# Expert layer of a hybrid encoder step: gate/up products with the weights stationary, downs and one-hot products by pair

## The chip, the core and the metric

One Trainium2 chip, one of its NeuronCores; everything runs in one launch. The metric is the time of the core in microseconds (us), smaller is better.

## The reference

One layer: adaLN, an input projection, an RWKV-7 branch and a gated linear attention branch, a merge, and then a hierarchical mixture of 32 experts on 544 rows (512 prompt, 32 sample) of 1024 numbers, all float32. The change concerns the experts only. Every row chooses two of the 32 experts:

```python
for e in range(N_EXPERTS):
    hid = jax.nn.silu(ht @ e_gate[e]) * (ht @ e_up[e])        # (T, 512)
    out = out + combine[:, e:e + 1] * (hid @ e_down[e])       # (T, 1024)
x = x + gt2 * out                                             # then the final RMS norm
```

The gate and up matrices of an expert are 1024x512, the down matrix 512x1024: 2 MB (a "unit") each, 96 units in all.

## The kernel before, in words

The stages before the experts (input projection, both branches, merge, `w_out`, router) are not touched, but for the layout of a few small tiles. The router ranks the rows of each expert and gives each a slot. A **round** does 64 slots (`BLK`) of every expert; with the inputs of the reference one round is enough. Experts go in 16 **pairs** (`NP`). For a pair, GpSimd gathers 128 rows from DRAM into `x_blk` (`gather`, L2124), 64 for each expert. Then, on TensorE (the loop is `a_round` of the tensor block, from L2754):

- `rows_turned` (products on L2672): eight 128x128 transposes; VectorE copies them to `x_t` (`rows_copied`, L3058), 8 blocks of [128 of the model dimension, 128 slots], in two buffers.
- `gate_up(e)` (L2711): the stationary operand is `x_t[:, k]` of the expert's 64 slots (128x64), the moving operand is 512 columns of gate or up weights. Gate goes to PSUM partitions 0 to 63, up to 64 to 127, 16 products in pairs of column halves. VectorE copies the result to `gu` (`gate_up_copied`, L3065).
- `hidden_turned(e)` (L2724): four 128x128 transposes of `gu`, so that the hidden dimension lies on the partitions; ScalarE makes the silu (L2485), VectorE multiplies by up (`hidden`, L3070) into `hid`.
- `down(e)` (L2736): stationary `hid[:, f]` (128x64), moving 512 columns of down weights, 8 products; the two halves of the 1024 outputs go to the two halves of the partitions. VectorE multiplies by the row's weight times `gt2` (`coef`, `down_scaled`, L3084), ScalarE rounds that to fp32r (L2491) and VectorE makes the rest (L3087).
- `rows_added(pair, j)` (L2689): for each of five row tiles, one-hot matrices (64 slots x 128 rows, made by `one_hots` on VectorE) times the two fp32r parts for both experts of the pair, 8 products; VectorE adds the result to `x2` (`rows_summed`, L3111). They are spread over the k loop of the next pair's odd `gate_up` (`PRODUCTS_AT`).
- The last pair has its own end: `last_down` (L2750), `last_added` (L3117), norm (`normed`, L3126, squares on ScalarE) and the stores (L2236).

The order on TensorE is written out by hand: `gate_up(e + 1)`, then `down(e)`, then `hidden_turned(e + 1)`. The units stream through eight buffers; SyncE's queue issues the load of unit n (L2025) once unit n - 8 has been used (`gu_mm`, `dn_mm`), and TensorE waits for `wg_in`, `wd_in`. A float32 product is carried out as two MATMUL instructions, each behind a LDWEIGHTS of its own; a product of fp32r operands is one of each.

Of the kernel before, what the change touches and what calls it, by code (L numbers as in the profile page):

```python
# [13 lines left out]
P = 128  # L14
# [25 lines left out]
def build(nc, I, O):  # L40
    ctx = ExitStack()
    with ctx:
# [1804 lines left out]
        tmp = Region(LOWER + 4 * D + 256, LOWER + MID - 4 * D)  # L1847
# [7 lines left out]
        ROW_WORDS = 2 * 5 * P + 4 * 512  # L1855
# [51 lines left out]
        E_LAST = NE - 2  # L1907
# [19 lines left out]
        gt2_h = Region(base + D).take(2, 512)  # L1927
# [13 lines left out]
        slot_w = route.take(2, NE)  # L1941
# [18 lines left out]
        tgt = small.take(NE)  # L1960
# [17 lines left out]
        act_g = low.take(4, BLK)  # L1978
        hid = low.take(4, BLK)
        gu = [Region(pos_oh_at + 512 * s).take(512) for s in range(2)]  # L1980
        after_units = Region(LOW_UNIT + 8 * D, rhs_at)
        moe_r = Region(LOWER, LOWER + ROW_WORDS)
        oh_t = moe_r.take(2, 5, P)
        y_parts = [[moe_r.take(512) for _ in range(2)] for _ in range(2)]
        after_r = Region(LOWER + ROW_WORDS, ARENA - 24 * D)
        x_t = [after_r.take(KD, 2 * BLK) for _ in range(2)]
        code_rows = [after_r.take(5, P), after_units.take(5, P)]
        y_full = after_units.take(512)
        consts_over = Region(summing_at, summing_at + 1200)
        coef = [consts_over.take(512) for _ in range(2)]  # L1990

        def y_of(e):

            return x_blk[:, 512 * (e % 2):512 * (e % 2) + 512] if e >= E_LAST else y_full

# [3 lines left out]
        STREAM = [("gate", 0), ("up", 0)]  # L1999
        for e in range(NE):  # L2000
            STREAM += [("gate", e + 1), ("up", e + 1)] * (e + 1 < NE) + [("down", e)]
# [14 lines left out]
        wg_in = [sem(f"wg_in{s}") for s in range(3)]  # L2016
        wd_in = [sem(f"wd_in{s}") for s in range(3)]
# [4 lines left out]
        def load_unit(sp, n):  # L2022
            kind, e = STREAM[n]
            source, landed = {"gate": (egate, wg_in), "up": (eup, wg_in), "down": (edown, wd_in)}[kind]
            sp.dma_start(weights_of(kind, e), source[e]).then_inc(landed[e % 3], 16)  # L2025
# [93 lines left out]
        def weights_kept(v, r, table):  # L2119
            v.wait_ge(slot_w_mm, r + 1)  # L2120
            nc.vector.tensor_copy(slot_w.rearrange("p a e -> p (a e)"), table[:, 0:2 * NE]).then_inc(slot_w_done, 1)
# [9 lines left out]
        gu_out = sem("gu_out")  # L2131
        gu_tr = sem("gu_tr")
# [11 lines left out]
        oh_done = sem("oh_done")  # L2144
        yh_done = sem("yh_done")
        yrest_done = sem("yrest_done")
        moe_mm = sem("moe_mm")
# [9 lines left out]
        DN_USES = [len(range(s, NE, 3)) for s in range(3)]  # L2157
        ADDS = 5 * (NP - 1)
        GU_USES = [len(range(s, NE, 3)) for s in range(3)]
# [14 lines left out]
        with nc.Block() as block:  # L2174
            @block.sync
            def _(sp):
# [24 lines left out]
                for s in range(2):  # L2201
                    for b in range(2):
                        sp.dma_start(gt2_h[BLK * b:BLK * b + BLK, s, :],
                                     mod_dram[s, 5 * D + 512 * b:5 * D + 512 * b + 512].partition_broadcast(BLK)
                                     ).then_inc(last_rows_in, 16)
# [8 lines left out]
                def a_round(r):  # L2214
                    if not first(r):
                        sp.wait_ge(dn_mm, r * NE)
                        sp.sem_inc(held, 1)
                        sp.wait_ge(y_final, r * 80)
                        sp.sem_inc(held, 1)
                        for n in range(8):  # L2220
                            load_unit(sp, n)
                    for n in range(8, len(STREAM)):
                        kind, e = STREAM[n - 8]
                        sp.wait_ge(dn_mm if kind == "down" else gu_mm, r * NE + (e + 1))
                        if n == len(STREAM) - 1:
                            sp.wait_ge(dn_mm, r * NE + (NE - 3))
                        load_unit(sp, n)
                    sp.wait_ge(gu_mm, r * NE + (NE - 1))
                    sp.sem_inc(held, 1)
                    sp.wait_ge(dn_mm, r * NE + (NE - 2))  # L2230
# [13 lines left out]
            def _(pool):  # L2244
# [46 lines left out]
                for b in range(2):  # L2291
                    half = slice(BLK * b, BLK * b + BLK)
                    i = iota_i[half, 0:NE].bitcast(I32)
                    step(pool.iota(i, pattern=[[int(CODE), NE]], base=int(CODE), channel_multiplier=1))
                    step(pool.tensor_copy(tgt[half], i))
# [14 lines left out]
                def a_round(r):  # L2310
                    if not first(r):
                        pool.wait_ge(idx_done, r * 2 + 2)
                        pool.wait_ge(x_tr9, r * NE)
                        pool.wait_ge(last_mm, r * 5)
# [7 lines left out]
            def _(act):  # L2322
# [138 lines left out]
                for k in range(2):  # L2461
                    nc.scalar.activation(code_rows[k][:, 0:4, :].rearrange("p i t -> p (i t)"), bank(6 + k), ACT.Copy
                                         ).then_inc(code_out, 1)
                for k in range(2):
                    nc.scalar.activation(code_rows[k][:, 4, :], bank(4)[:, k * P:(k + 1) * P], ACT.Copy
                                         ).then_inc(code_out, 1)

                def coef_of_prompt(r, e):
                    s = e % 2
                    if e >= 2:  # L2470
                        act.wait_ge(y_done, r * NE + (e - 1))
                    else:
                        act.wait_ge(slot_w_done, r + 1)
                    if e == 0 and first(r):
                        act.wait_ge(last_rows_in, 64)
                    nc.scalar.activation(coef[s], gt2_h[:, 0, :], ACT.Copy, scale=slot_w[:, 0, e:e + 1]
                                         ).then_inc(coef_half, 1)

                def a_round(r):
                    for e in range(2):  # L2480
                        coef_of_prompt(r, e)
                    for e in range(NE):
                        s = e % 2
                        act.wait_ge(gu_tr, r * NE + (e + 1))
                        nc.scalar.activation(act_g, psum[2][:, 0, :].rearrange("p (f t) -> p f t", f=4)[:, :, 0:BLK],  # L2485
                                             ACT.Silu).then_inc(silu_done, 1)
                        if 1 <= e < NE - 1:
                            coef_of_prompt(r, e + 1)
                        if e < E_LAST:
                            act.wait_ge(y_done, r * NE + (e + 1))  # L2490
                            nc.scalar.activation(y_parts[s][0], y_full, ACT.Copy).then_inc(yh_done, 1)  # L2491
# [12 lines left out]
            def _(pe):  # L2504
# [153 lines left out]
                for k in range(2):  # L2658
                    for i in range(5):
                        row = bank(6 + k)[:, i * P:(i + 1) * P] if i < 4 else bank(4)[:, k * P:(k + 1) * P]  # L2660
                        m = mm(row, code[:, k, i:i + 1].broadcast_to([P, P]), ident, start=True, stop=True)
                m.then_inc(code_mm, 1)

                def rows_turned(r, p):
                    pe.wait_ge(x_in9, r * (NP * 16) + 16 * p + 16)
                    for h in range(2):
                        if p:
                            pe.wait_ge(x_t9, r * NE + (2 * p + h - 1))
                        elif not first(r):
                            pe.wait_ge(x_t9, r * NE)  # L2670
                        for k in range(4):
                            m = nc.tensor.transpose(psum[h][:, 0, k * P:(k + 1) * P],  # L2672
# [3 lines left out]
                PRODUCTS_AT = [1, 3, 5, 7]  # L2676

                def rows_added(r, pair, j):
                    n = 5 * pair + j
                    if j == 0:  # L2680
                        pe.wait_ge(yrest_done, r * E_LAST + (2 * pair + 2))
                        pe.wait_ge(oh_done, r * NE + (2 * pair + 2))
                    if n:
                        pe.wait_ge(moe_added, r * ADDS + n)
                    for h in range(2):
                        for part in range(2):
                            for b in range(2):
# [6 lines left out]
                def gate_up(r, e):  # L2694
                    s = e % 2
                    pair = e // 2 - 1 if s and e >= 3 else None
                    if e == NE - 1:
                        for j in range(5):
                            rows_added(r, pair, j)
                    pe.wait_ge(x_t9, r * NE + (e - s + 2))  # L2700
                    pe.wait_ge(wg_in[e % 3], r * (32 * GU_USES[e % 3]) + 32 * (e // 3) + 32)
                    if e >= 2:
                        pe.wait_ge(gu_out, r * NE + (e - 1))
                    elif not first(r):
                        pe.wait_ge(x3_done, r * 5)
# [489 lines left out]
```

## Time and profile before

| | us |
|---|---|
| median of 3 runs | 1511.84 (1511.11 to 1514.94) |
| the profiled execution, its own time | 1509.26 |
| its span in the profile | 1507.5 |
| issue of the first unit, start of the first gate/up product in that span | 961.7, 993.2 |
| mean granted TensorE clock | 0.975 |
| busy: TensorE matmul / VectorE / ScalarE | 1400.7 / 722.2 / 473.9 |

A granted clock of 1 is 2.4 GHz, 0.5 is 1.2 GHz. The expert stage is the stretch from 991 us to the end; a pair takes 30.67 us there.

### The profile page before, as it was taken

The numbers are of one execution on the slowest core, as the hardware profiler recorded it, in microseconds if no ns is written. First come the engines' busy times: TensorE is split into PE (matmuls) and PEld (weight loads), VectorE is DVE, ScalarE is ACT, GpSimd is POOL, SyncE is SP. The second block draws the span as 40 slices with busy tenths as digits, with TensorE's granted clock in tenths as the row PEclk, the third lists the DMA queues.
The fourth block names the chain that finished last, engine by engine and source line by source line (L and its number), as shares of the span: only waits on it lengthen the run. The fifth ranks groups of instructions, "written<-read, shape, count | busy, mean of one in ns | idle before, by whom it ended". The sixth has DMA issues, their size and how long they took to land. (4 is left out here: it accounts for less than half of the span.)

```text
span 1507.5 us, 31643 instructions
## 1 busy us (share of the span) xinstructions
PE 1400.7 (93%) x14017; PEld 1015.6 (67%) x14017; DVE 722.2 (48%) x1184; ACT 473.9 (31%) x764; POOL 167.2 (11%) x200
## 2 busy tenths in 40 slices
PE   5899999999999998888879999799999999999986
PEld 1778999999998987777779998653333333333332
DVE  3322134652235456556555666624555554554545
ACT  2333345554554543333335442110100110011002
POOL 2000000010112124324201101000000000000000
PEclk9999999999999998999999999789999999999988
DMA  8656422234432210000422461499999999999951
GB/s 313 195 187 222 139 72 71 83 110 130 124 90 60 68 44 11 4 5 4 135 56 74 163 213 63 198 407 426 427 426 427 425 427 426 427 426 425 426 232 61
DMA packets 124510, 310.01 MB, mean 206 GB/s; under 512 B 12407, under 2 KB 97617, under 8 KB 109010
## 3 DMA queue, kind: packets, MB, share of 16 engines
q1 hardware_dynamic: 113680, 285.07, 49.8%
q10 hardware_dynamic: 7522, 15.57, 2.9%
q0 software_dynamic: 3168, 7.30, 1.3%
q8 instruction: 113, 1.85, 0.5%
q14 instruction: 27, 0.22, 0.0%
HBM read 299.06 MB, written 12.79 MB: 207 GB/s over the span
## 5 line engine op out<-in xcount | busy, mean ns | idle before, releaser
L838 PE MATMUL bank<-upper2end 128*128 128x272 f32 x3168 | 419.2, 291 | 5.4 <-DVE upper2end L1079 5.4
L838 PEld LDWEIGHTS bank<-upper2end 128*128 128x128 f32 x3168 | 403.4, 189 | 27.5 <-issue 26.2
L1056 DVE TENSOR_TENSOR upper2end<-upper,upper2end 128x1024 fp32r<-128x1024 f32 x66 | 81.7, 1238 | 286.3 <-ACT upper2end L604 286.2
L2711 PE MATMUL bank<-upper7b 128*64 128x512 f32 x784 | 208.0, 603 | 1.0 <-DVE upper7b L3058 1.0
L2491 ACT ACTIVATE upper_r7b<-lower 128x512 fp32r<-128x512 f32 x30 | 18.9, 629 | 407.4 <-DVE lower L3084 407.4
L3111 DVE TENSOR_TENSOR lower<-lower,bank 128x1024 f32<-128x1024 f32 (+1 forms) x75 | 91.4, 1218 | 97.2 <-PE bank L2689 97.2
L2711 PEld LDWEIGHTS bank<-upper7b 128*64 128x64 f32 x784 | 57.7, 137 | 96.9 <-issue 93.0
L2689 PEld LDWEIGHTS bank<-upper_r7b 64*128 64x128 f32 x600 | 52.5, 191 | 86.5 <-DVE lower L3111 58.6
L2689 PE MATMUL bank<-upper_r7b 64*128 64x512 f32 x600 | 93.2, 430 | 18.0 <-DVE lower L3111 9.6
L2543 PE MATMUL bank<-upper_r 128*128 128x272 f32 x768 | 103.0, 294 | 3.2 <-DVE upper_r L2958 3.2
L2543 PEld LDWEIGHTS bank<-upper_r 128*128 128x128 f32 x768 | 99.4, 191 | 5.9 <-DVE upper_r L2790 3.6
L2736 PE MATMUL bank<-upper7b,lower 128*64 128x512 f32 x368 | 83.5, 595 | 0.0
L2711 PE MATMUL bank<-lower,upper7b 128*64 128x512 f32 x240 | 81.4, 602 | 0.0
L604 ACT ACTIVATE upper2end<-upper 128x1024 fp32r<-128x1024 f32 x66 | 69.6, 1054 | 11.0 <-ACT upper L633 6.5
L2124 POOL DMA_INDIRECT lower<-expert_in,lower x16 | 16.0, 1001 | 427.0 <-PE bank L2672 385.1
L3084 DVE TENSOR_TENSOR lower<-bank,lower 128x512 f32<-128x512 f32 x32 | 22.1, 692 | 79.3 <-PE bank L2736 79.3
L2736 PEld LDWEIGHTS bank<-upper7b,lower 128*64 128x64 f32 x368 | 25.4, 137 | 47.1 <-issue 45.7
L2575 PE MATMUL bank<-upper_r 128*128 128x512 f32 x192 | 48.0, 407 | 0.0
L3065 DVE COPY lower<-bank 128x512 f32<-128x512 f32 x32 | 22.0, 688 | 49.6 <-PE bank L2711 49.6
L1442 ACT ACTIVATE upper<-bank 128x512 f32<-128x512 f32 x36 | 21.5, 597 | 74.2 <-DVE upper L1518 74.1
L789 PE MATMUL bank<-lower 128*32 128x512 f32 x184 | 29.3, 703 | 15.7 <-DMA lower<-in_w_ada 15.7
L2575 PEld LDWEIGHTS bank<-upper_r 128*128 128x128 f32 x192 | 36.7, 194 | 9.3 <-issue 1.1
(412 smaller groups left out, 1904.0 us busy)
## 6 DMA issues: line engine op xcount, KB each, us to landing
upper7b<-in_expert_w_gate SPq DMA_DIRECT2D x25, 2048.0 KB, 20.3
upper7b<-in_expert_w_up SPq DMA_DIRECT2D x24, 2048.0 KB, 21.9
upper7b<-in_expert_w_down SPq DMA_DIRECT2D x23, 2048.0 KB, 17.0
upper<-in_w_in SPq DMA_DIRECT2D x66, 512.0 KB, 3.9
lower<-in_w_ada SPq DMA_DIRECT2D x23, 1024.0 KB, 5.0
lower<-in_expert_w_down SPq DMA_DIRECT2D x9, 2048.0 KB, 16.3
lower<-in_expert_w_up SPq DMA_DIRECT2D x8, 2048.0 KB, 23.3
lower<-in_expert_w_gate SPq DMA_DIRECT2D x7, 2048.0 KB, 20.8
```

The costliest lines, as they stand in the source:

```text
L604: nc.scalar.activation(w_high[u % 2], w_slot[u % 2], ACT.Copy).then_inc(w_high_done, 1)
L789: m = mm(acc[32 * b:32 * b + 32, :], c_t[:, k, :], w[:, b * 512:(b + 1) * 512], start=k == 0, stop=k == KD - 1)
L838: m = mm(psum[s][:, c, 0:HALF], w_part[s][:, k, :], h_part[:, k, c * HALF:(c + 1) * HALF], start=k == 0 and w_part is w_high and h_part is ...
L1056: ve.tensor_tensor(w_rest[u % 2], w_slot[u % 2], w_high[u % 2].bitcast(F32), ALU.subtract).then_inc(w_split, 1)
L2543: m = mm(psum[s][:, c, 0:HALF], w[s][:, k, :], cols(y[b][:, k], c), start=k == 0 and w is wb_high and y is y_high, stop=k == KD - 1 and w ...
L2575: m = mm(psum[OUT_BANKS[i]][:, b, :], m_part[:, k, t], w[:, b * 512:(b + 1) * 512], start=k == 0 and m_part is m_high and w is not wo_rest[k],
L2689: m = nc.tensor.matmul(psum[3][:, b, :], oh_t[half, h, AT[j], :], y_parts[h][part][half, :], start=h + part == 0, stop=h + part == 2)
L2711: m = nc.tensor.matmul(psum[s][64 * b:64 * b + 64, 1, :], x_t[(e // 2) % 2][:, k, s * BLK:(s + 1) * BLK], w[:, k, :], start=k == 0, stop=k ...
L2736: m = nc.tensor.matmul(psum[2][64 * b:64 * b + 64, 1, :], hid[:, f, :], w[:, f, b * 512:(b + 1) * 512], start=f == 0, stop=f == 3)
L3065: ve.tensor_copy(gu[s], psum[s][:, 1, :]).then_inc(gu_out, 1)
L3084: ve.tensor_tensor(y_of(e), psum[2][:, 1, :], coef[s], ALU.mult).then_inc(y_done, 1)
L3111: ve.tensor_tensor(x2[0:n, j, :], x2[0:n, j, :], psum[3][0:n].rearrange("t b c -> t (b c)"), ALU.add).then_inc(moe_added, 1)
```

## The change

Gate and up weights become the stationary operand (128x128 blocks, their columns taken with a step of four words), the 64 slots of `x_t` the moving one. The products then come out with the hidden dimension on the partitions: `gu`, its copy and `hidden_turned` go; silu reads PSUM, `hidden` multiplies with PSUM. A `gate_up` is 64 products with 64 moving columns in place of 16 with 512.

```diff
-                    gate_and_up = weights_of("gate", e), weights_of("up", e)
-                    for k in range(KD):
-                        if pair is not None and e < NE - 1 and k in PRODUCTS_AT:
-                            rows_added(r, pair, PRODUCTS_AT.index(k))
-                        for b, w in enumerate(gate_and_up):
-                            m = nc.tensor.matmul(psum[s][64 * b:64 * b + 64, 1, :],
-                                                 x_t[(e // 2) % 2][:, k, s * BLK:(s + 1) * BLK], w[:, k, :],
-                                                 start=k == 0, stop=k == KD - 1)
+                    for n, kind in enumerate(("gate", "up")):
+                        pe.wait_ge(*landed(r, kind, e))
+                        w = weights_of(kind, e).rearrange("p k (n q) -> p k q n", q=4)
+                        for q in range(4):
+                            at = 4 * BLK * n + BLK * q
+                            for k in range(KD):
+                                m = nc.tensor.matmul(bank(2 + s)[:, at:at + BLK], w[:, k, q, :],
+                                                     x_t[:, k, s * BLK:(s + 1) * BLK], start=k == 0, stop=k == KD - 1)
+                            if q == 3:
+                                m.then_inc(gu_mm, 1)
+                            if e >= 2 and 8 * s + 4 * n + q in PRODUCTS_AT:
+                                rows_added(r, e // 2 - 1, PRODUCTS_AT.index(8 * s + 4 * n + q))
```

The two downs of a pair are done together, expert 0 on partitions 0 to 63 and expert 1 on 64 to 127, both halves of the outputs in one two-bank tile; scaling, rounding and the rest are then done once per pair on 128x1024. The one-hot matrix holds 128 slots, and a tile needs 4 products in place of 8:

```diff
+                    for f in range(4):
+                        for b in range(2):
+                            for s in range(2):
+                                m = nc.tensor.matmul(psum[2][64 * s:64 * s + 64, b, :], hid[s][:, f, :],
+                                                     w[s][:, f, b * 512:(b + 1) * 512], start=f == 0, stop=f == 3)
...
-                    for h in range(2):
-                        for part in range(2):
-                            for b in range(2):
-                                half = slice(BLK * b, BLK * b + BLK)
-                                m = nc.tensor.matmul(psum[3][:, b, :], oh_t[half, h, AT[j], :],
-                                                     y_parts[h][part][half, :], start=h + part == 0,
-                                                     stop=h + part == 2)
+                    for part in range(2):
+                        for b in range(2):
+                            m = nc.tensor.matmul(psum[3][:, b, :], oh_t[:, j * P:(j + 1) * P],
+                                                 y_parts[part][:, b * 512:(b + 1) * 512], start=part == 0,
+                                                 stop=part == 1)
```

The order on TensorE, the order of the units and the pair's end become:

```diff
+                    for p in range(NP):
+                        gate_up(r, 2 * p)
+                        gate_up(r, 2 * p + 1)
+                        if p < P_LAST:
+                            rows_turned(r, p + 1)
+                        down(r, p)
+                    for j in range(5):
+                        last_rows_added(r, j)
...
+        for e in range(0, NE, 2):
+            STREAM += [("gate", e), ("up", e), ("gate", e + 1), ("up", e + 1), ("down", e), ("down", e + 1)]
...
+                PRODUCTS_AT = [4, 6, 8, 10, 12]
```

Beside that `x_t` has one buffer, each of the eight unit buffers a semaphore of its own, a gate unit is released as soon as the gate products are done, `gt2` is broadcast to 128 partitions (two loads of 512 KB for four of 128 KB), and the last pair goes the way of the others: rounded and rest parts made by halves (`last_scaled`, `last_rounded`), then four fp32r products for each tile (`last_rows_added`) in place of `last_down`'s float32 ones.

## Rows read from the trace of the kernel before

**Rows 1.** The page: what the DMA engines moved, GB/s in 40 equal slices of the span.
```profile
GB/s 313 195 187 222 139 72 71 83 110 130 124 90 60 68 44 11 4 5 4 135 56 74 163 213 63 198 407 426 427 426 427 425 427 426 427 426 425 426 232 61
```

**Rows 2.** Busy time by stretch, core 0: one pair of the expert stage.
```profile
core 0: us, PE busy (x) PEld busy (x) DVE busy (x) ACT busy (x) POOL busy (x), PEclk, DMA share, GB/s
...
1100.80:1131.47 30.67, 29.87 (x154) 11.74 (x152) 15.85 (x21) 3.02 (x6) 0.99 (x1) 1.00 1.01 427
```

**Rows 3.** Waits of SyncE's queue, 1020 to 1440 us: us in total, times, longest.
```profile
SPq L2025 <- PE bank L2711: 285.3, 28, 13.0
```

**Rows 4.** Issue to landing of the units (L2025): 1000 to 1200, then 1300 to 1456 us.
```profile
DMA to landing us min/median/max: 15.2/20.9/26.3
...
DMA to landing us min/median/max: 13.0/18.5/24.0
```

**Rows 5.** Timeline of PE (start, us, what, xcount): first gate/up, transposes, down, hidden transposes.
```profile
993.21 7.09 PE L2711 MATMUL bank<-upper7b 128*64 128x512 f32 x32 [1.01 <-DVE upper7b L3058]
...
1100.80 1.16 PE L2672 MATMUL bank<-lower 128*128 128x128 f32 x8
1101.89 3.65 PE L2736 MATMUL bank<-lower 128*64 128x512 f32 x16
1105.47 0.75 PE L2724 MATMUL bank<-lower 128*128 128x128 f32 x4
```

**Rows 6.** Groups of PE and VectorE in the pair of Rows 2: one-hot products and their adds.
```profile
line engine op names shapes xcount | busy us, mean ns | idle before us <-releasers
...
L2689 PE MATMUL bank<-upper_r7b 64*128 64x512 f32 x42 | 6.4, 415 | 0.8 <-DVE upper_r7b L3087 0.5 <-DVE lower L3111 0.3
L3111 DVE TENSOR_TENSOR lower<-lower,bank 128x1024 f32<-128x1024 f32 x4 | 4.9, 1220 | 5.6 <-PE bank L2689 5.6
```

**Rows 7.** Router burst, 36 columns moving: its loads in the timeline, then by line (min/median/max ns).
```profile
938.92 1.64 PEld L2604 LDWEIGHTS bank<-lower 128*128 128x128 f32 x14
...
L2604 PEld LDWEIGHTS bank<-lower x15: 192/192/193, 938.8 to 940.4; 128*128 128x128 f32 x15
```

**Rows 8.** Timeline of a burst of float32 loads whose products move 128 columns.
```profile
386.76 0.98 PEld L950 LDWEIGHTS bank<-lower,upper 128*128 128x128 f32 x8
```

**Rows 9.** Groups by line and shape: fp32r products of 272 columns.
```profile
L838 PE MATMUL bank<-upper2end 128*128 128x272 f32 x3168 | 419.2, 291 | 5.4 <-DVE upper2end L1079 5.4
```

**Rows 10.** Timeline of PE: fp32r products of 512 columns, weights 128x128.
```profile
940.52 8.60 PE L2575 MATMUL bank<-upper_r 128*128 128x512 f32 x36
```

**Rows 11.** Timeline of the last hidden tile: silu on ScalarE, product on VectorE.
```profile
1482.99 0.38 ACT L2485 ACTIVATE lower<-bank 128x256 f32<-128x256 f32 x1 [26.55 <-PE bank L2724]
...
1483.41 0.42 DVE L3070 TENSOR_TENSOR lower<-lower,bank 128x256 f32<-128x256 f32 x1 [0.39 <-ACT lower L2485]
```

**Rows 12.** Timeline after a down: scaling on VectorE, rounding on ScalarE.
```profile
1443.07 0.69 DVE L3084 TENSOR_TENSOR lower<-bank,lower 128x512 f32<-128x512 f32 x1 [2.27 <-PE bank L2736]
1443.79 0.63 ACT L2491 ACTIVATE upper_r7b<-lower 128x512 fp32r<-128x512 f32 x1 [18.05 <-DVE lower L3084]
```

**Rows 13.** Timeline of VectorE at the end: last down scaled, first tile added.
```profile
1487.92 0.69 DVE L3084 TENSOR_TENSOR lower<-bank,lower 128x512 f32<-128x512 f32 x1 [3.43 <-PE bank L2736]
1489.93 1.22 DVE L3117 TENSOR_TENSOR lower<-lower,bank 128x1024 f32<-128x1024 f32 x1 [1.31 <-PE bank L2750]
```

**Rows 14.** Busy time by stretch (columns of Rows 2): router, end, and RWKV recurrence.
```profile
967.00:991.00 24.00, 20.57 (x98) 19.94 (x96) 7.47 (x43) 2.76 (x5) 1.76 (x2) 0.51 1.01 423
...
1459.00:1472.00 13.00, 9.04 (x36) 4.84 (x38) 4.58 (x4) 0.00 (x0) 0.00 (x0) 0.50 0.00 0
...
586.00:731.00 145.00, 122.77 (x4714) 110.37 (x4712) 87.21 (x180) 54.03 (x103) 54.60 (x42) 1.00 0.04 12
```

**Rows 15.** Timeline of PE at the end of the router, at the lower clock.
```profile
980.17 4.48 PE L2092 MATMUL bank<-lower 128*128 128x32 f32 x20 [2.12 <-DVE lower L3047]
...
986.59 4.61 PE L2661 MATMUL bank<-lower 128*128 128x128 f32 x20
```

More of the change, by code:

```diff
@@ L1940, in build @@
         code = route.take(2, 5)
[L1941 removed]
+        slot_w = route.take(2, NP)
         oh_both = route.take(2, 5, NE)
@@ L1977, in build @@
         low = Region(base + 4 * D, LOW_UNIT)
-        act_g = low.take(4, BLK)
-        hid = low.take(4, BLK)
-        gu = [Region(pos_oh_at + 512 * s).take(512) for s in range(2)]
+        hid = [low.take(4, BLK) for _ in range(2)]
         after_units = Region(LOW_UNIT + 8 * D, rhs_at)
+        act_g = after_units.take(4 * BLK)
+        coef = Region(base + D).take(D)
+        y_full = Region(pos_oh_at).take(D)
         moe_r = Region(LOWER, LOWER + ROW_WORDS)
[L1983 to L1988, printed above, removed]
+        oh_t = moe_r.take(5 * P)
+        y_parts = [moe_r.take(D) for _ in range(2)]
+        x_t = Region(LOWER + ROW_WORDS + 2 * D, ARENA - 24 * D).take(KD, 2 * BLK)
         consts_over = Region(summing_at, summing_at + 1200)
-        coef = [consts_over.take(512) for _ in range(2)]
-        def y_of(e):
-            return x_blk[:, 512 * (e % 2):512 * (e % 2) + 512] if e >= E_LAST else y_full
+        code_rows = [consts_over.take(T) for _ in range(2)]
         UNIT = 4 * D
@@ L1998, in build @@
         UNIT_AT = [experts_at + n * UNIT for n in range(1, 7)] + [LOW_UNIT + UNIT, LOW_UNIT]
-        STREAM = [("gate", 0), ("up", 0)]
-        for e in range(NE):
-            STREAM += [("gate", e + 1), ("up", e + 1)] * (e + 1 < NE) + [("down", e)]
+        STREAM = []
+        for e in range(0, NE, 2):
+            STREAM += [("gate", e), ("up", e), ("gate", e + 1), ("up", e + 1), ("down", e), ("down", e + 1)]
         unit_no = {kind_e: n for n, kind_e in enumerate(STREAM)}
@@ L2156, in build @@
         ROUNDS_MAX = (T + BLK - 1) // BLK
-        DN_USES = [len(range(s, NE, 3)) for s in range(3)]
         ADDS = 5 * (NP - 1)
-        GU_USES = [len(range(s, NE, 3)) for s in range(3)]
+        P_LAST = NP - 1
+        LAST_BANKS = (3, 0, 1, 2, 3)
         NORM_AT = {j: (2 * j + 1, 2 * j + 2) for j in range(5)}
@@ L2479, in a_round, with coef_of_prompt @@
-                def a_round(r):
[L2480 to L2491, printed above, removed]
+                def coef_of_prompt(r, p):
+                    if p:
+                        act.wait_ge(y_done, r * P_LAST + p)
+                    else:
+                        act.wait_ge(slot_w_done, r * 2 + 2)
+                        if first(r):
+                            act.wait_ge(last_rows_in, 32)
+                        else:
+                            act.wait_ge(y_last, r * 2)
+                    nc.scalar.activation(coef, gt2_b[:, 0, :], ACT.Copy, scale=slot_w[:, 0, p:p + 1]
+                                         ).then_inc(coef_half, 1)
@@ L2658, in _ @@
                 for k in range(2):
-                    for i in range(5):
-                        row = bank(6 + k)[:, i * P:(i + 1) * P] if i < 4 else bank(4)[:, k * P:(k + 1) * P]
-                        m = mm(row, code[:, k, i:i + 1].broadcast_to([P, P]), ident, start=True, stop=True)
+                    for j, n in TILES:
+                        row = bank(6 + k)[:, j * P:(j + 1) * P] if j < 4 else bank(4)[:, k * DEC:(k + 1) * DEC]
+                        m = mm(row, code[:, k, AT[j]:AT[j] + 1].broadcast_to([P, P]), ident[:, 0:n], start=True,
+                               stop=True)
                 m.then_inc(code_mm, 1)
@@ L2718, in hidden_turned @@
-                def hidden_turned(r, e):
-                    s = e % 2
-                    pe.wait_ge(gu_out, r * NE + (e + 1))
-                    if e == 0 and first(r):
-                        pe.wait_ge(code_out, 4)
-                    for f in range(4):
-                        m = nc.tensor.transpose(psum[2][:, 0, f * P:(f + 1) * P],
-                                                gu[s].rearrange("t (p k) -> t k p", p=P)[:, f, :], ident)
-                    m.then_inc(gu_tr, 1)
-                def down(r, e):
-                    pe.wait_ge(hid_done, r * NE + (e + 1))
-                    pe.wait_ge(wd_in[e % 3], r * (16 * DN_USES[e % 3]) + 16 * (e // 3) + 16)
-                    if e >= 1:
-                        pe.wait_ge(y_done, r * NE + e)
-                    w = weights_of("down", e)
-                    for f in range(4):
-                        for b in range(2):
-                            m = nc.tensor.matmul(psum[2][64 * b:64 * b + 64, 1, :], hid[:, f, :],
-                                                 w[:, f, b * 512:(b + 1) * 512], start=f == 0, stop=f == 3)
-                    m.then_inc(dn_mm, 1)
@@ L2747, in last_down @@
                     pe.sem_inc(held, 1)
-                    for b in range(2):
-                        half = slice(BLK * b, BLK * b + BLK)
-                        m = nc.tensor.matmul(psum[j % 4][0:n, b, :], oh_t[half, i, AT[j], 0:n].bitcast(F32),
-                                             y_of(E_LAST + i)[half, :], start=i == 0, stop=stop)
-                    return m
+                    for part, ready in enumerate((yh_last, yrest_last)):
+                        for b in range(2):
+                            if j == 0:
+                                pe.wait_ge(ready, r * 2 + (b + 1))
+                            m = nc.tensor.matmul(psum[LAST_BANKS[j]][:, b, :], oh_t[:, j * P:(j + 1) * P],
+                                                 y_parts[part][:, b * 512:(b + 1) * 512], start=part == 0,
+                                                 stop=part == 1)
+                    m.then_inc(last_mm, 1)
                 def a_round(r):
```

276 lines of the change are left out of this document (131 added, 145 removed).

## The prediction, as put on record before the changed kernel was run

> **What bounds the kernel now.** I looked first for the stage that the change touches. From 991 us on the experts run, a third of the span, and there the page shows the DMA engines flat at 425 to 427 GB/s [rows 1], which looks like a bound by weight traffic. The busy times by stretch show more: one pair takes 30.67 us, the pairs before and after it take the same, TensorE is busy 29.87 us of it and its clock is whole [rows 2]. So TensorE, too, is full. The waits tell which of the two leads: the queue that issues the units waits for the gate/up products, 285.3 us in 420 [rows 3], while no wait of TensorE for a load is listed. The landings say the same: a unit lands 20.9 us after its issue early in the stage and 18.5 us late in it [rows 4]; the loads gain on TensorE a little. TensorE sets the pair at 30.67 us, and DMA is just behind: 26.3 us against 24.0 us at most over some ten pairs [rows 4] puts it some 0.2 to 0.3 us a pair lower, about 30.4. That is the floor: whatever TensorE saves in a pair, hardly more than 0.3 us of it can show, and whatever it gains in work shows in full.
>
> **The pair before, on TensorE.** A gate/up is 32 instructions in 7.09 us to the end of the last, some 6.9 us to the next instruction; two of them run side by side in the two column halves, so a pair of instructions takes 0.43 us [rows 5]. Transposes 1.09, a down 3.58 from start to start, hidden transposes 0.75 or 0.7 to the next start [rows 5]. Twice 6.9, 3.5 and 0.7, and 1.1, make 23.3 us; the remaining 7.4 are the five one-hot groups (6.4 busy [rows 6]) and the switches around them.
>
> **Gate/up after: the term that decides.** Per expert 64 products of 64 moving columns, each float32 and so two instructions: 128 loads of 128x128 weights and 128 matmuls, 256 of each per pair. Before it was 64 instructions per pair, two at a time. The arithmetic is the same, but the array was filled from the long side; now the load has the 128 columns and the matmul only 64. What such a load costs is in the router: there float32 weights of 128x128 meet only 36 moving columns. 14 loads take 1.64 us, the last one 0.192, so they follow at (1.64 - 0.19) / 13 = 0.111 us at the full clock [rows 7]. With 128 columns moving the pace is (0.98 - 0.19) / 7 = 0.113 [rows 8]. From 36 to 128 columns nothing changes: the load is the bound, and the matmul hides under it. 64 lies between, so I take 0.112: 256 x 0.112 = 28.7 us per pair, against 13.8 before. Bounds: the least that rows 7 leave is 0.107 (27.4 us); above, the fp32r products pace at 419.2 / 3168 = 0.132 with 272 columns [rows 9], of which I allow 0.125 (32.0 us), because the new loads step over four words and no row with many such loads shows their price when nothing longer hides it.
>
> At one place a page speaks differently. The Trainium skill, "TensorE: Matmul & The Clock Gate", section "Back-to-back issue gap", has a stream of load and matmul pairs at about 81 ns with 128 moving columns; the trace has 0.113 us for the same columns in float32 [rows 8], and the measurement decides. By the page's figure gate/up would be an estimated 20.7 us per pair.
>
> **The other parts, per pair.**
> - Hidden transposes (8 instructions, 1.4 us) and two copies of `gu` go. VectorE's work falls, but it was busy only 15.85 of 30.67 us [rows 2]: worth nothing by itself.
> - One-hot products: 20 instructions of 512 columns in place of 40 that ran in pairs. Full-height fp32r products pace at (8.60 - 0.40) / 35 = 0.234 [rows 10]: 4 are 0.94, with the switch 0.98, five 4.9 us. They wait for the adds (1.22 us [rows 6]), but two blocks of eight products, 3.6 us, lie between two groups: hidden. The first comes after five blocks, 9 us; scaling, rounding and rest of 128x1024 take about twice 0.69, 0.63 and 0.69 [rows 12], 4 us: hidden.
> - Transposes of the next inputs, 1.1 us, unchanged. `x_t` has one buffer now; its copies (1.3 us) run under the down of 7 us.
> - Down: 16 products, 32 instructions, again two at a time: twice the 16 of [rows 5], 6.95 us. Before it, `hid` of the second expert must be there: silu 0.38, product 0.42 [rows 11], with drain and hops 1.25 us after the last gate/up product, of which the transposes cover 1.1: 0.2 us.
> - Loads: six units per pair in 41.8 us are 300 GB/s, below what ran before; they land early. The wider `gt2` rows put 0.5 MB ahead of two units (1.2 us), and those are needed 30 us later: nothing. `coef` on ScalarE stands before the first silu, but both are due only 14 us into the stage.
>
> Sum: 28.7 + 4.9 + 1.1 + 0.2 + 6.95 = 41.85 us a pair, 11.2 more than 30.67. The first pair has no one-hot products: 36.9.
>
> **The ends.** The stage starts as before, at 993.2 [rows 5]; router and code products keep their loads. The last down ends at 993.2 + 36.9 + 15 x 41.85 = 1657.9. Before, the first add came 2.0 us after it [rows 13]; now two scalings, a rounding, two rests by halves and two more products stand in the chain: 0.69 + 0.69 + 0.04 + 0.69 + 0.69 [rows 12] and some 0.6, 3.4 us. From the first add to the end is 1507.5 - 1489.9 = 17.6 us [rows 13], led by adds and norms that don't change. The old kernel's bare one-hot groups at the lower clock before its last gate/up (1459 to 1472 [rows 14]) go, which the count of pairs contains. Span 1657.9 + 3.4 + 17.6 = 1678.9. The profiled execution took 1509.26 for a span of 1507.5: 1680.7; the median lies 2.6 higher: **1683 us**.
>
> **Rivals.**
> - *The loads hide, DMA is the floor (faster).* If the 64-column matmul set the pace (0.43 us is four times 128 columns, so 64 take about 0.055) or one load served both instructions, gate/up would be some 14 us, TensorE's pair 27 to 28 us, under the 30.4 of DMA. It decides from 0.068 us per instruction down. Then 96 units and the gathers, 209 MB at 427 GB/s, run from the first issue at 962 to 1453; a down, the new chain and the end (28 us) give a span of 1481, 1486 us in all. Against it: each of the matmuls in rows 7 and 8 has its own load, at 0.111. Chance 0.05.
> - *A pace between, about 0.08.* Gate/up 20.7, pair 33.8, by the same sum 1558 us. The page's 81 ns above is this case, worked out here from the pair of rows; rows 7 speak against it. Chance 0.05.
> - *The clock falls.* Before the experts TensorE worked without a stop on loads with 32 columns moving, 967 to 991 us, at a granted clock of 0.51 [rows 14]: 20 such instructions took 4.48 us, 0.22 each [rows 15]. The clock was whole again only after 20 products of 128 columns [rows 15]. The new gate/up is between: as many cycles of load as two of matmul. If the clock stays at 1.2 GHz, gate/up is 256 x 0.215 = 55 us, with products and downs partly at half speed a pair is some 74: about 2195 us. Against it: in the RWKV recurrence thousands of short products, down to 32 columns, with matmuls busy 123 of 145 us, kept 1.00 [rows 14]; and each pair ends in 7 us of dense downs. Chance 0.10, of a mild form (some pairs) within it.
>
> **How the numbers follow.** The forecast has 0.80. Its range: 0.107 takes 16 x 256 x 0.005 = 20 us off, smaller waits 8 more; 0.125 adds 53 and waits 8: 1655 to 1745. The rivals lie outside and hold the 0.20 left. A measurement of this kernel can tell about 0.3% (4.5 us) from no change. Slower: 0.80 + 0.05 + 0.10, less a little; faster: 0.05; a pace that lands on no change: 0.01.
>
> **What would show it.** Right: the pair is 41 to 43 us; gate/up matmuls start every 0.112 us, and weight loads are busy nearly all of gate/up where they were 11.7 of 30.7; the GB/s fall from 427 to about 310; the queue waits for TensorE still more; granted clock 1.00. Wrong: a pace of 0.055 with GB/s at 427 (first rival), 0.08 (second), PEclk 0.5 in gate/up (third). If the pace is 0.112 and the pair still over 43, a wait that I put at nothing is there: before a down for `hid`, or before a one-hot group for `yrest_done`. A pace far above 0.125 at a full clock would mean that the four-word step of the weights costs.

## The result, and the profile after

The changed kernel takes 2265.25 us (median of 4 runs, 2263.54 to 2266.86) against 1511.97: the ratio is 1.498, 95% interval 1.495 to 1.500. The profiled execution took 2266.47 us for a span of 2264.7. The forecast was 1683, in a range of 1655 to 1745; the direction was right, and the size was wrong by 582 us.

The page of the changed kernel: span, busy time, clock and DMA in 40 slices, and the costliest groups (line engine op out<-in, shapes, xcount | busy us, mean ns | idle before).

```profile
span 2264.7 us, 36761 instructions
PE 2170.1 (96%) x16641; PEld 1948.5 (86%) x16641; DVE 681.0 (30%) x1078; ACT 472.5 (21%) x735; POOL 180.5 (8%) x200
...
PEclk9999999999999899955555555555555555555556
...
L2703 PEld LDWEIGHTS bank<-upper7b 128*128 128x128 f32 x3072 | 728.7, 329 | 20.7 <-issue 8.9
L2703 PE MATMUL bank<-upper7b 128*128 128x64 f32 x3072 | 723.8, 435 | 1.0 <-DVE upper7b L3044 1.0
```

The weight loads, busy two thirds of the span before, are busy 86% of a longer one, and the mean clock in the expert stage is 0.56 (1500 to 2000 us). At first sight this is the forecast's third rival (the clock falls, 2195 us). From the first input transposes of one pair to those of the next is a pair, and the starts of the groups between give its parts:

```profile
1446.41 1.92 PE L2686 MATMUL bank<-lower 128*128 128x128 f32 x8
...
1524.89 1.91 PE L2686 MATMUL bank<-lower 128*128 128x128 f32 x8
```

```profile
1502.86 2.05 PE L2733 MATMUL bank<-upper_r7b 128*128 128x512 f32 x4
1504.71 7.52 PE L2703 MATMUL bank<-upper7b,lower 128*128 128x64 f32 x32
...
1526.73 8.60 PE L2720 MATMUL bank<-upper7b,lower 128*64 128x512 f32 x32
1535.26 18.93 PE L2703 MATMUL bank<-upper7b 128*128 128x64 f32 x80
```

A pair is 78.5 us, where it was 30.67 [rows 2] and 41.85 was forecast. From start to start a one-hot group is 1.85 us (forecast 0.98), the down 8.5 (6.95), the transposes 1.8 (1.1). Taking these off, 78.5 - 9.25 - 8.5 - 1.8 = 58.9 us are left for gate/up, forecast 28.7. So 30 of the 36.6 us that the pair is over its forecast are gate/up.

The row that decides what slowed it stands right behind a down, where the clock had just been raised. Busy times by stretch (core 0: us, PE, PEld, DVE, ACT, POOL busy, clock, DMA share, GB/s), and the timeline of the loads in the first of the two:

```profile
1536.00:1539.80 3.80, 3.80 (x18) 3.80 (x18) 1.83 (x2) 2.10 (x2) 0.00 (x0) 1.00 0.94 310
1541.00:1603.00 62.00, 62.00 (x252) 60.07 (x251) 6.51 (x6) 0.38 (x1) 0.00 (x0) 0.50 0.37 142
```

```profile
1535.94 4.06 PEld L2703 LDWEIGHTS bank<-upper7b 128*128 128x128 f32 x17
```

At a granted clock of 1.00 the loads follow at (4.06 - 0.33) / 16 = 0.233 us, not 0.112. At 0.50 they take the same: 32 instructions in 7.52 us, (7.52 - 0.44) / 31 = 0.228. (The two figures differ by how the runs are cut; over 80 instructions that begin in the first stretch it is (18.93 - 0.44) / 79 = 0.234.) A load whose time doesn't change with the clock isn't slow because of the clock. What sets these loads apart from those of [rows 7] and [rows 8] is their step of four words. That the step makes them slow is theory S below; theory C, its rival, is that the fallen clock does.

### The profile page after: what moved, and what is told of

Its sections match the earlier page's. It is cut to its first block, busy times and chain, and to the rows that moved or that the text cites. A ratio compares the mean times of both kernels' runs of the same rounds, so it can differ in the third digit from the quotient of the medians.

```text
span 2264.7 us, 36761 instructions
## 1 busy us (share of the span) xinstructions
PE 2170.1 (96%) x16641; PEld 1948.5 (86%) x16641; DVE 681.0 (30%) x1078; ACT 472.5 (21%) x735; POOL 180.5 (8%) x200
## 4 chain that ended last, share of the span: by engine, by line
PE 64%; DVE 1%; ACT 0%; issue 0%; ACTq 0%; DVEq 0%
PE bank L2703 42%; PE bank L2733 6%; PE bank L2720 6%; PE bank L2556 4%; PE bank L2588 2%; PE bank L2686 1%; PE bank L2540 1%; PE bank L2617 0%; DVE upper7b L3112 0%; DVE lower L3103 0%; PE bank L2082 0%; PE bank L2090 0%; PE bank L2537 0%; PE bank L2674 0%; PE bank L2603 0%
## 5 line engine op out<-in xcount | busy, mean ns | idle before, releaser
L2703 PEld LDWEIGHTS bank<-upper7b 128*128 128x128 f32 x3072 | 728.7, 329 | 20.7 <-issue 8.9
L2703 PE MATMUL bank<-upper7b 128*128 128x64 f32 x3072 | 723.8, 435 | 1.0 <-DVE upper7b L3044 1.0
L2703 PEld LDWEIGHTS bank<-upper7b,lower 128*128 128x128 f32 x1024 | 243.5, 329 | 7.1 <-issue 3.2
L2703 PE MATMUL bank<-upper7b,lower 128*128 128x64 f32 x1024 | 241.9, 435 | 0.0
L2733 PE MATMUL bank<-upper_r7b 128*128 128x512 f32 x300 | 154.1, 665 | 0.0
L2125 POOL DMA_INDIRECT lower<-expert_in,lower x16 | 29.0, 1810 | 1079.7 <-PE bank L2686 991.0
L2720 PE MATMUL bank<-upper7b,lower 128*64 128x512 f32 x384 | 101.6, 689 | 0.0
L2733 PEld LDWEIGHTS bank<-upper_r7b 128*128 128x128 f32 x300 | 88.7, 326 | 14.5
L3050 DVE TENSOR_TENSOR lower<-lower,bank 128x256 f32<-128x256 f32 x32 | 13.5, 421 | 255.7 <-ACT lower L2484 255.7
L2488 ACT ACTIVATE upper_r7b<-lower 128x1024 fp32r<-128x1024 f32 x15 | 15.9, 1057 | 165.2 <-DVE lower L3078 165.2
L2588 PEld LDWEIGHTS bank<-upper_r 128*128 128x128 f32 x192 | 36.6, 194 | 9.2 <-issue 1.1
```

Source lines behind the costliest of these rows:

```text
L2125: pool.indirect_dma_start(x_blk, None, h2_dram, bass.IndirectOffsetOnAxis(ap=as_u32(x_idx[:, p:p + 1]), axis=0), bounds_check=T - 1, oob_i ...
L2588: m = mm(psum[OUT_BANKS[i]][:, b, :], m_part[:, k, t], w[:, b * 512:(b + 1) * 512], start=k == 0 and m_part is m_high and w is not wo_rest[k],
L2703: m = nc.tensor.matmul(bank(2 + s)[:, at:at + BLK], w[:, k, q, :], x_t[:, k, s * BLK:(s + 1) * BLK], start=k == 0, stop=k == KD - 1)
L2720: m = nc.tensor.matmul(psum[2][64 * s:64 * s + 64, b, :], hid[s][:, f, :], w[s][:, f, b * 512:(b + 1) * 512], start=f == 0, stop=f == 3)
L2733: m = nc.tensor.matmul(psum[3][:, b, :], oh_t[:, j * P:(j + 1) * P], y_parts[part][:, b * 512:(b + 1) * 512], start=part == 0, stop=part == 1)
```

## The experiments

**unit_step.** The weight blocks are taken with a step of one word, and the down weights are loaded in the rows that match:

```diff
-        edown = I["expert_w_down"][0].rearrange("e (p k) f -> e p k f", p=P)
+        edown = I["expert_w_down"][0].rearrange("e (k p) f -> e p k f", p=P)
...
-                        w = weights_of(kind, e).rearrange("p k (n q) -> p k q n", q=4)
+                        w = weights_of(kind, e).rearrange("p k (q n) -> p k q n", q=4)
```

> The changed kernel with the weight blocks taken with a step of one word (hidden index q*128 + partition) and the down weights loaded in the rows that match, so the result is the reference's. Theory S (the step): a load of 128 columns with a step of four words takes 0.233 us at either clock, and the lower clock only follows from TensorE mostly loading. Then the load here is 0.112 us, the clock in gate/up may hold at 1.00, a pair is 42 us, about 1685 us in all; if the clock falls all the same, loads are 0.213 us and a pair is some 74 us, about 2200 us. Theory C (the clock): the fall of the clock alone made the loads slow, whatever the step: about 2200 us or more, granted clock near 0.5 in gate/up. A pace of 0.112 with a clock of 1.00 is for S; 0.213 with 0.5 leaves both open.

Measured: 1678.42 us, ratio to before 1.1105 (1.1075 to 1.1135). One pair by stretch, then its loads and its parts in the timeline:

```profile
1104.43:1145.81 41.38, 41.38 (x318) 35.50 (x318) 12.98 (x14) 2.87 (x4) 0.99 (x1) 1.00 0.81 312
```

```profile
1320.01 7.12 PEld L2703 LDWEIGHTS bank<-upper7b 128*128 128x128 f32 x63
...
1311.35 1.09 PE L2686 MATMUL bank<-lower 128*128 128x128 f32 x8
1312.44 7.09 PE L2720 MATMUL bank<-lower 128*64 128x512 f32 x32
1319.46 9.14 PE L2703 MATMUL bank<-upper7b 128*128 128x64 f32 x80
1328.41 1.17 PE L2733 MATMUL bank<-upper_r7b 128*128 128x512 f32 x4
1329.42 3.68 PE L2703 MATMUL bank<-upper7b 128*128 128x64 f32 x32
```

The loads follow at (7.12 - 0.19) / 62 = 0.112 us, the clock is 1.00 and the pair 41.38. This edit is worth 587 us (2265.25 - 1678.42), what the clock gives back included. Every term of the forecast's sum stands here: transposes 1.09, down 7.02, a one-hot group 1.01, and 28.2 for gate/up. The edit also has the down weights loaded in 4 KB pieces; the next kernels separate that from the step.

**step2, step3.** The changed kernel, down weights loaded as in it, with other steps. The hidden numbers are then taken in an order (for three words: from columns that overlap) that doesn't belong to the down weights; no work is left out.

```diff
-                        w = weights_of(kind, e).rearrange("p k (n q) -> p k q n", q=4)
+                        w = weights_of(kind, e).rearrange("p k (h n q) -> p k h q n", h=2, q=2)
...
-                                m = nc.tensor.matmul(bank(2 + s)[:, at:at + BLK], w[:, k, q, :],
+                                m = nc.tensor.matmul(bank(2 + s)[:, at:at + BLK], w[:, k, q // 2, q % 2, :],
```

and for three words

```diff
-                        w = weights_of(kind, e).rearrange("p k (n q) -> p k q n", q=4)
+                        w = weights_of(kind, e)
...
-                                m = nc.tensor.matmul(bank(2 + s)[:, at:at + BLK], w[:, k, q, :],
+                                m = nc.tensor.matmul(bank(2 + s)[:, at:at + BLK], w[:, k, 32 * q:32 * q + 3 * P - 2:3],
```

> The changed kernel with the weight blocks taken with a step of two words in place of four; the order of the hidden numbers then does not match the down weights, the amount of work is the same. Theory S in its proportional form (a load takes step x 0.058 us, and not under 0.107): about 0.117 us per instruction, pair 43 us, about 1705 us. Theory S in its all-or-nothing form (every step over one word costs): 0.233 us, about 2265 us as with four. Theory C: no difference to four words, about 2265 us, clock 0.5 in gate/up.

> The changed kernel with weight blocks at a step of three words (they overlap, the contents are not the reference's; the amount of work is the same). If the load takes 0.0583 us per word of step (0.118 at two, 0.233 at four): 0.175 us, gate/up 44.8 us. With the clock at 1.00 a pair is some 57.5 us, about 1925 us; if the clock falls, one-hot products and downs run partly at half speed, some 61 us, about 1985 us. If the cost went by powers of two (banks of the memory): three costs as much as one or two, 0.112 to 0.118, about 1690 us.

Measured: step2 1701.49 us, ratio 1.125 (1.121 to 1.129); step3 2125.91 us in one run. Loads in the timelines of step2, then of step3 right after a down and a few us later, and the clock of step3 in the same two places:

```profile
1289.87 8.21 PEld L2703 LDWEIGHTS bank<-upper7b 128*128 128x128 f32 x69
```

```profile
1198.47 2.69 PEld L2703 LDWEIGHTS bank<-upper7b 128*128 128x128 f32 x15
...
1202.82 11.42 PEld L2703 LDWEIGHTS bank<-upper7b 128*128 128x128 f32 x53
```

```profile
1198.30:1200.90 2.60, 2.60 (x17) 2.60 (x17) 1.48 (x2) 1.56 (x2) 0.00 (x0) 1.00 0.71 195
1201.50:1214.00 12.50, 12.50 (x60) 12.50 (x61) 0.15 (x1) 0.00 (x0) 0.00 (x0) 0.51 0.81 320
```

Two words: (8.21 - 0.19) / 68 = 0.118 us. The down weights are loaded here as in the changed kernel, so their load isn't the cause: two words in place of four alone give back 564 us. Three words: (2.69 - 0.26) / 14 = 0.174 at the full clock, on the expected 0.175, and this rules out that only powers of two matter. At the lower clock it is (11.42 - 0.33) / 52 = 0.213, as the router's loads [rows 15]. This reads as two bounds side by side, of which the larger counts: one that goes with the step and not with the clock, and one that goes with the clock and not with the step: 0.213 at 0.50, and half of that, 0.107, at 1.00, where a step of one word was measured at 0.112. The time of step3 was expected at 1985 if the clock fell; it fell (0.65 from 1100 to 1600 us) and made the loads 0.213, where the expectation had left them at 0.175: missed by 141 us.

**wide_step4, wide_unit.** Each gate/up product moves all 128 slots of the pair in place of 64; only the half that belongs to the expert is read afterwards. Loads and their number are the same.

```diff
-                                m = nc.tensor.matmul(bank(2 + s)[:, at:at + BLK], w[:, k, q, :],
-                                                     x_t[:, k, s * BLK:(s + 1) * BLK], start=k == 0, stop=k == KD - 1)
+                                m = nc.tensor.matmul(bank(2 + n)[:, 2 * BLK * q:2 * BLK * (q + 1)], w[:, k, q, :],
+                                                     x_t[:, k, :], start=k == 0, stop=k == KD - 1)
```

> The changed kernel, step of four words, but each gate/up product moves all 128 slots of the pair and half of its output is not read: twice the columns under each load, same loads, result the reference's. The two experts share two banks, which adds a wait of 1.2 us per pair. Theory S: the load stays 0.233 us, gate/up 59.6 us, pair some 75 us even at a clock of 1.00, about 2190 us; it can be a little under the changed kernel, for the one-hot products and downs then run at the full clock. Theory C: more columns moving keep the clock at 1.00, the loads go at 0.112 us, pair 43 to 44 us, about 1710 us.

> As wide_step4, with the weight blocks at a step of one word and the matching down weights; result the reference's. Theories S and C both: clock 1.00, load 0.112 us, gate/up 28.8 us, pair 43 to 44 us, about 1710 us. It is the check that 128 moving columns hide under the load: if unit_step is at 1.00 and this equals it within 25 us, the columns are free; if unit_step is at 0.5 and this at 1.00, the clock follows the columns that move.

Measured: wide_step4 2194.08 us, ratio 1.451 (1.446 to 1.455); wide_unit 1698.11, ratio 1.123 (1.119 to 1.127). wide_step4 by stretch over five pairs, and a piece of its timeline:

```profile
1130.00:1500.00 370.00, 364.83 (x1594) 334.86 (x1593) 65.38 (x72) 14.70 (x21) 4.94 (x5) 0.98 0.46 175
```

```profile
1204.61 1.04 PE L2687 MATMUL bank<-lower 128*128 128x128 f32 x8
1205.70 7.09 PE L2720 MATMUL bank<-upper7b,lower 128*64 128x512 f32 x32
1212.72 13.57 PE L2703 MATMUL bank<-upper7b 128*128 128x128 f32 x57
```

This is the experiment that parts the two causes. The clock is 0.98 in place of some 0.56, downs and transposes are back at 7.0 and 1.1 us, and the loads still go at (13.57 - 0.4) / 56 = 0.235. Theory C's 1710 us is out by 480. What the clock itself costs the changed kernel is what came back: 2265 - 2194 = 71 us, and some 20 us more that the added waits hide (the two experts of a pair share two banks here, so a `gate_up` waits until `hidden` has read the one before). These 20 us are what wide_unit takes over unit_step (1698.11 - 1678.42). Its timeline shows them before the second `gate_up` of a pair, and the products at unit_step's pace:

```profile
1204.12 9.20 PE L2703 MATMUL bank<-upper7b,lower 128*128 128x128 f32 x80
...
1221.51 2.02 PE L2703 MATMUL bank<-upper7b 128*128 128x128 f32 x16 [0.98 <-issue]
```

80 instructions take 9.20 us, 9.14 in unit_step: twice the columns are free under the load, as expected.

**unit_turned_product.** unit_step, with the input transposes as plain float32 products with the identity; the stationary operand, at a step of eight words, is the same.

```diff
-                            m = nc.tensor.transpose(bank(h)[:, k * P:(k + 1) * P],
-                                                    x_blk.rearrange("t (p k) -> t k p", k=KD)[:, 4 * h + k, :], ident)
+                            m = nc.tensor.matmul(bank(h)[:, k * P:(k + 1) * P],
+                                                 x_blk.rearrange("t (p k) -> t k p", k=KD)[:, 4 * h + k, :], ident,
+                                                 start=True, stop=True)
```

> unit_step with the eight input transposes of a pair as float32 products with the identity; their stationary operand, x_blk at a step of eight words, stays the same. As transposes they pace at 0.113 us in spite of that step. If the law of the step holds for products only, each of the 16 instructions takes 8 x 0.0583 = 0.467 us: 7.5 us in place of 1.1, pair 47.8 us, about 1780 us. If instead the cost belonged to the weight buffers and not to the step, 16 x 0.112 = 1.8 us, pair 42.1 us, about 1690 us.

Measured: 1748.9 us, ratio 1.158 (1.154 to 1.162), between the two expectations. Its loads in the timeline, at a clock of 1.00:

```profile
1316.62 3.67 PEld L2686 LDWEIGHTS bank<-lower 128*128 128x128 f32 x15
```

(3.67 - 0.34) / 14 = 0.238 us: eight words cost what four cost, not twice that. The law is therefore not proportional to the end: 0.118, 0.174, 0.233, 0.238 for steps of 2, 3, 4 and 8 words. That is 0.058 us for every word of step up to four and flat from there, which is what a memory would give that is read in lines of 16 bytes: 128 columns touch 64, 96, 128 and 128 lines, an estimated 1.82 ns each. At a step of one, 32 lines would be 0.058 us, and the bound that goes with the clock, 0.107, covers it. And the same operand that costs 0.238 us in a product goes at (1.09 - 0.27) / 7 = 0.117 as a transpose (unit_step, eight in 1.09 us). The lines are a reading that fits five points; a pattern that would part step and line (short runs with gaps) wasn't tried.

The pair is 44.24 us, 2.86 over unit_step's; over 15 pairs that is 43 of the 70 us between the two kernels. Another 24 lie in the first two `gate_up`, before any one-hot product. First all their matmuls in this kernel, its loads and its busy times in a stretch of them, then the same 256 matmuls in unit_step:

```profile
998.09 53.15 PE L2704 MATMUL bank<-upper7b 128*128 128x64 f32 x256 [0.78 <-DVE upper7b L3045]
```

```profile
1001.86 48.33 PEld L2704 LDWEIGHTS bank<-upper7b 128*128 128x128 f32 x226
```

```profile
1001.00:1053.00 52.00, 52.00 (x244) 52.00 (x244) 0.84 (x2) 3.20 (x4) 0.00 (x0) 0.50 0.54 200
```

```profile
993.04 28.80 PE L2703 MATMUL bank<-upper7b 128*128 128x64 f32 x256 [1.01 <-DVE upper7b L3044]
```

The loads, the columns and the step of one word are the same, but here the clock was 0.50 for 52 us, and the loads followed at (48.33 - 0.33) / 225 = 0.213 us. It was whole again from 1055 us, behind the 16 turned products that come next, and stayed at 1.00 in all later pairs. Before it fell, TensorE had done the turned products (0.238 us a load) at 1.00, where unit_step had done transposes; that these made it fall is not shown.

**moving_pairs.** The other parts of the change without gate/up: slots stationary and weights moving as before, the copy and the hidden transposes back, but downs side by side, 128-slot one-hot products and the new last pair.

```diff
-                        w = weights_of(kind, e).rearrange("p k (n q) -> p k q n", q=4)
-                        for q in range(4):
...
+                    for k in range(KD):
+                        if e >= 2 and 8 * s + k in PRODUCTS_AT:
+                            rows_added(r, e // 2 - 1, PRODUCTS_AT.index(8 * s + k))
+                        if 8 * s + k == TURNED_AT:
+                            hidden_turned(r, e - 1)
+                        for b, w in enumerate(both_w):
+                            m = nc.tensor.matmul(bank(2 + s)[64 * b:64 * b + 64, :],
+                                                 x_t[:, k, s * BLK:(s + 1) * BLK], w[:, k, :],
+                                                 start=k == 0, stop=k == KD - 1)
...
+                    if s:
+                        if e >= 2:
+                            rows_added(r, e // 2 - 1, 4)
+                        hidden_turned(r, e)
```

> The other parts of the change alone: gate/up as before (slots stationary, weights moving, copy and hidden transposes back), downs of a pair side by side, 128-slot one-hot products, the new last pair. Result the reference's. Both theories say that nothing of the loss is in these parts. TensorE: 13.8 (gate/up) + 1.4 (hidden transposes) + 6.5 (one-hot with switches) + 1.1 + 6.95 + 0.3 = 30.1 us a pair, so that DMA at about 30.4 becomes the bound; the bare one-hot groups at the lower clock before the last gate/up go (about 18 us). About 1497 us, ratio 0.990; range 1490 to 1508. Rival: the serial chain copy, transposes, silu, product, down is not covered, 1.5 us more a pair: about 1520 us.

Measured: 1490.17 us, ratio to before 0.987 (0.984 to 0.990), at the low edge of what was expected. It beats both kernels, the one before by 1.3%. Groups of PE in one pair, and the last pair in the timeline:

```profile
L2709 PE MATMUL bank<-upper7b 128*64 128x512 f32 x64 | 15.0, 600 | 0.0
L2737 PE MATMUL bank<-upper7b,lower 128*64 128x512 f32 x32 | 7.1, 595 | 0.3 <-DVE lower L3071 0.3
L2750 PE MATMUL bank<-upper_r7b 128*128 128x512 f32 x20 | 6.0, 421 | 0.0
```

```profile
1454.65 1.20 PE L2750 MATMUL bank<-upper_r7b 128*128 128x512 f32 x4
1455.68 0.63 PE L2723 MATMUL bank<-lower 128*128 128x128 f32 x4
1457.48 7.09 PE L2737 MATMUL bank<-lower 128*64 128x512 f32 x32 [1.16 <-DVE lower L3071]
1466.02 5.49 PE L2766 MATMUL bank<-upper_r7b 128*128 128x512 f32 x20 [1.46 <-ACT upper_r7b L2495]
```

The pair of these groups (from 1186.27 us) is 29.5 us, and TensorE waits no longer than 0.3 us in it. The one-hot groups no longer stand bare before the last gate/up at the lower clock, as they did at 1459 to 1472 us [rows 14]. That DMA is close behind TensorE shows too: a unit lands 19.4 us after its issue at 1000 to 1100 us and 27.4 us after it at 1300 to 1400 (medians), and from 1300 to 1450 us one product waits for its weights (waits: us in total, times, longest):

```profile
PE bank L2709 <- DMA upper7b<-in_expert_w_up: 1.9, 1, 1.9
```

The pair with this wait took 33.3 us, at a mean clock of 0.95; thirteen pairs took 29.84 us in the mean (from 1038.66 to 1426.61 us).

## Why the prediction was wrong, point by point

- **What bounds the kernel.** Right: TensorE leads, DMA is just behind. The floor of 30.4 us a pair was near the pace of the DMA (the forecast's 209 MB at 427 GB/s are 30.6 us a pair) but no limit on sixteen pairs: moving_pairs ran most of its pairs in 29.5 us on the buffers' lead and had to wait for weights once. "Hardly more than 0.3 us of it can show" was wrong by this: 0.8 us a pair did show.
- **Gate/up, the term that failed.** The count, 256 loads and 256 matmuls one after the other, was right, and so was "the load is the bound, and the matmul hides under it" (wide_unit: twice the columns, the same pace). Mis-sized was the price of one load: "I take 0.112", with 0.125 as the upper bound "because the new loads step over four words". It measured 0.233. The 0.112 came from rows whose operand has a step of one word, and unit_step shows it there. The experts of the kernel before did hold stationary operands at four and eight words, but only in transposes [rows 5], where the price doesn't show; the bound above had no row with such a step behind it, and should then have been wide. This term alone is 30 us a pair, 480 us of the 582.
- **The clock.** The rival was right in what it saw and had its cause wrong. Its case, loads at a step of one word with 64 columns moving, ran at 1.00 all through the stage in unit_step. It isn't excluded, though: for 52 us of unit_turned_product the same loads and columns ran at 0.50 and 0.213 us a load, the rival's price, and cost 24 us. What decides between the two is open. With the same columns under loads of 0.174 and 0.233 us the engine falls to 1.2 GHz in gate/up and comes back in the downs. The fall then costs the one-hot groups (1.85 for 1.01), the first part of each down and the transposes; that is the other 6 us a pair, some 100 us; wide_step4 got 91 of them back (71, and the 20 of its waits). The rival's 2195 us is near the result by luck: it had 0.215 per load from the clock, where 0.233 came from the step.
- **The other parts.** Down 7.0, one-hot group 1.01, transposes 1.09, copies and rounding hidden: all as summed. unit_step's 1678 is 5 us under the forecast's 1683, and shows its sum for a kernel that the diff isn't.
- **The fast rival and the one of 0.08 us** are excluded: loads are the bound already at a step of one word, at 0.112. (By the forecast's own sum the second is 1555 us and not 1558; nothing hangs on it.)
- **What would show it.** "A pace far above 0.125 at a full clock would mean that the four-word step of the weights costs": this is what the rows at 1536 us show.

Put together: the change turned 7 us of two-at-a-time products per expert into 128 serial loads and then made each load twice as long. The first is +11 us a pair with the gain of the other parts taken off (166 us in all, the ratio 1.11 of unit_step), the second +37 us a pair with what the clock takes (587 us in all). The other parts alone gain 20 us (1510.2 - 1490.2).

The Trainium skill has a rule for the failed term, in "SBUF — State Buffer", section "Door 1: The DMA port swizzle (why `[64,N]` ≈ `[32,N]`)": SBUF is read in lines of 16 bytes, and full bandwidth needs at least two hits in a line. The runs agree in kind: two words of step cost 5% (0.118 for 0.112), three cost 55%, four 108%. The rule has no price in it, but by it a step of four words, one hit in a line, was a rival to be weighed. The same note has it that how far one can stride for free depends on the type, four words for float32; that does not hold for these loads, for at four words the price is full.

## What to carry to other kernels

Before weights become the stationary operand, count loads and not flops: a float32 product is two 128-column loads of 0.112 us each, and with up to 128 moving columns the array waits for them. Keep the stationary operand at a step of one word, two at most, and choose the order of a hidden dimension by loading the next weights to match: the down units of unit_step landed in a median of 9.0 us, those of step2, loaded the old way, in 8.8, and neither was waited for. When a granted clock falls in a new kernel, look for a stretch in which it is still whole: if the instructions are as slow there, the clock isn't what makes them slow.

## What was not expected of the hardware

- A float32 load of 128x128 weights takes 0.112, 0.118, 0.174, 0.233 and 0.238 us for steps of 1, 2, 3, 4 and 8 words, at a granted clock of 1.00. At 0.50, one and three words both cost 0.213 and four words the same 0.23 as at 1.00.
- The same operand at eight words costs 0.238 us as a product's load and is not seen in a transpose, which goes at 0.117.
- 128x128 loads one after the other with 64 columns moving lost the clock at 0.174 and 0.233 us each; with 128 columns moving they kept it (0.98) at 0.235. At a step of one word with 64 columns both were seen: 1.00 and 0.112 us all through unit_step, and 0.50 and 0.213 us for 52 us of unit_turned_product.
